# Constant products put between the tensor engine's waits at the head of a two-block transformer kernel

## What is computed

```python
c_act = jax.nn.silu(c)
for l in range(DEPTH):
    mod = (c_act @ ada_w[l] + ada_b[l])[:, None, :]
    sh1, sc1, gt1, sh2, sc2, gt2 = jnp.split(mod, 6, axis=-1)
    h = rms_norm(x, norm_mix[l]) * (1.0 + sc1) + sh1
    x = x + gt1 * hybrid_mixer(h, w_in[l], ...)      # begins with proj = h @ w_in
    ...
```

## Time and profile before

| | |
|---|---|
| Median of three runs | 3062.19 us (3061.9 to 3067.84) |
| The profiled execution: its own time | 3064.68 us |
| Its span, first to last instruction | 3062.9 us |
| PE busy | 2978.7 us, 97% of the span |
| DVE busy | 2351.1 us, 77% |
| Mean granted clock of TensorE | 0.988 of full |

### The profile page before, as it was taken

How to read it: one execution, slowest core, us unless ns; L and a number is a source line. 1 busy time by engine, 2 the same in 40 slices (tenths; PEclk the granted TensorE clock), 3 DMA queues, 4 the chain that set the end, 5 groups by cost and what they waited for, 6 DMA issues and landing times.

```text
span 3062.9 us, 49634 instructions
## 1 busy us (share of the span) xinstructions
PE 2978.7 (97%) x20726; PEld 2665.8 (87%) x20726; DVE 2351.1 (77%) x2670; ACT 1637.7 (53%) x1613; POOL 74.3 (2%) x83
## 2 busy tenths in 40 slices
PE   7999999999999999999999999999989999998999
PEld 7998999999888788788887888899979988986898
DVE  7978698848675888989888888689687646658576
ACT  3445443445553777777777777643334424435543
POOL 0002000000010000000000000000000000100000
PEclk8999999999999999999999999999999999999999
DMA  8650487735303799999999999845325553541353
GB/s 357 255 192 11 176 316 304 264 121 188 142 16 124 280 362 369 362 368 368 364 368 358 371 365 371 305 153 185 130 94 196 181 177 139 205 165 42 129 187 123
DMA packets 130027, 703.09 MB, mean 230 GB/s; under 512 B 11184, under 2 KB 15552, under 8 KB 74048
## 3 DMA queue, kind: packets, MB, share of 16 engines
q1 hardware_dynamic: 118816, 650.30, 58.0%
q0 software_dynamic: 6880, 48.24, 3.9%
q10 hardware_dynamic: 4160, 2.12, 0.3%
HBM read 698.50 MB, written 1.07 MB: 228 GB/s over the span
## 4 chain that ended last, share of the span: by engine, by line
PE 89%; DVE 6%; ACT 2%; DMA 1%; issue 1%; SPq 0%; ACTq 0%; DVEq 0%
PE banks L532 20%; PE banks L533 20%; PE banks L534 20%; PE banks L542 7%; PE banks L543 4%; PE banks L475 3%; DMA ring<-in_wall 1%; DVE big L1446 1%; DVE ring_low L1446 1%; PE banks L643 1%; PE banks L485 1%; PE banks L891 1%; DVE tail L1446 1%; ACT parts L2562 1%; PE banks L555 1%
## 5 line engine op out<-in xcount | busy, mean ns | idle before, releaser
L1446 DVE TENSOR_TENSOR ring_low<-ring,parts 128x2048 fp32r<-128x2048 f32 x589 | 1341.5, 2287 | 281.4 <-ACT parts L2562 252.1
L532 PE MATMUL banks<-parts 128*128 128x256 f32 (+1 forms) x3360 | 1063.1, 316 | 4.2 <-ACT big L2733 2.2
L2562 ACT ACTIVATE parts<-ring 128x2048 fp32r<-128x2048 f32 x253 | 484.7, 1916 | 731.7 <-PE banks L534 495.4
L2668 ACT ACTIVATE parts<-ring 128x2048 fp32r<-128x2048 f32 x336 | 644.7, 1919 | 215.3 <-DMA ring<-in_wall 210.2
L534 PE MATMUL banks<-parts,ring_low 128*128 128x256 f32 x2464 | 694.1, 282 | 0.0
L532 PEld LDWEIGHTS banks<-parts 128*128 128x128 f32 x3360 | 634.7, 189 | 44.7 <-issue 3.3
L533 PE MATMUL banks<-tail_parts,parts 128*128 128x256 f32 x2032 | 573.3, 282 | 0.0
L534 PEld LDWEIGHTS banks<-parts,ring_low 128*128 128x128 f32 x2464 | 465.9, 189 | 0.0
L533 PEld LDWEIGHTS banks<-tail_parts,parts 128*128 128x128 f32 x2032 | 383.2, 189 | 1.9 <-issue 1.9
L542 PE MATMUL banks<-tail_parts,parts 128*128 128x512 f32 x1008 | 354.9, 394 | 1.6 <-DVE big L1496 1.1
L534 PE MATMUL banks<-parts,tail_parts 128*128 128x512 f32 x896 | 352.6, 394 | 0.0
(11 more groups left out here) (478 smaller groups left out, 3771.6 us busy)
## 6 DMA issues: line engine op xcount, KB each, us to landing
ring<-in_wall SPq DMA_DIRECT2D x616, 1024.0 KB, 6.5
big<-in_wall POOLq DMA_DIRECT2D x40, 1024.0 KB, 5.5
big<-in_w_k POOLq DMA_DIRECT2D x1, 2048.0 KB, 8.3
big<-in_w_v POOLq DMA_DIRECT2D x1, 2048.0 KB, 14.5
big<-bias_table ACTq DMA_DIRECT2D x2, 1024.0 KB, 7.2
constants<-in_con SPq DMA_DIRECT2D x1, 1249.5 KB, 9.0
x<-in_x SPq DMA_DIRECT2D x1, 1024.0 KB, 6.8
big<-big POOLq DMA_DIRECT2D x16, 64.0 KB, 4.8
```

Of the source, the lines that this page charges most:

```text
L532: pe.matmul(o, high, in_high, start=start, stop=False, **kw)
L1446: return ve.tensor_tensor(out, a, b, op)
L2562: act(parts(w_high(room, n), UNIT), ring[n % RING][:, :], ACT.Copy).then_inc(sem("w_high"), 1)
L2668: act(parts(slot_at(q), UNIT), ring[r][:, :], ACT.Copy).then_inc(sem("x_high"), 1)
```

## The change

`ada()` gets a helper that multiplies `EPS_ONES` by itself into bank 5, which nothing reads there (each product starts its own sum and ends it). 24 such products stand ahead of everything, six ahead of the wait for unit 1, and six ahead of each wait for the units 4, 5, 6 and 7: 54 products, 108 records. Nothing else is changed.

```diff
+            def keep_busy(count):
+
+                for _ in range(count):
+                    pe.matmul(bank[5][:, 0:P], EPS_ONES[:, :], EPS_ONES[:, :], start=True, stop=True)
+
             def ada():
 
+                pe.wait_ge(sem("eps_set"), 1)
+                keep_busy(24)
                 for n in range(FIRST):
+                    if n == 1:
+                        keep_busy(6)
                     if n == 2:
                         norm(0, 7)
+                    if n > 3:
+                        keep_busy(6)
                     pe.wait_ge(sem("weighted"), (n + 1) * KT)
                     for t in range(2):
                         for chain in range(2):
```

## The result

The changed kernel takes 3068.49 us in the median of 20 runs (3063.38 to 3075.48), the kernel before 3063.01 in 20 (3058.5 to 3067.84). The medians differ by 5.5 us; the ratio, estimated from all executions, is 1.0015, with a 95% interval of 1.0009 to 1.0021: 2.8 to 6.4 us slower, and clear of noise. In the experiments further down one execution of the kernel before, of 29, took 10867.86 us at a mean granted clock of 0.509, and no ratio counts it. The profiled execution took 3070.84 us, its span is 3069.0 and its mean granted clock 0.985.

What follows compares the result with a forecast made beforehand. The first slice's head delays the end in full, limited by DVE's weighing and PE's low-clock norm. PE then becomes the limit: +5.0 us, 0.8 of it from the norm, projections 0; 3062.2 + 5.0 = 3067.2, range 3062.8 to 3069.8.

Steps and rivals of the forecast that it cites:

- The opening burst: First 24 products: wait for x, run from 9.0 to 16.8; unit 0 done at 17.7, unit 2 weighed from 17.8.
- Absorbed by the idle time: Ahead of `modulation`: DVE's 3.54 us idle takes nearly all of a 3.4 us delay; `modulation` comes +0.8 us later.
- Units 4 to 7: After the norm: groups at the lower clock make PE the limit; unit 7 done at 45.1 instead of 39.9.
- The first projection: End of the head: 3.24 us of copy and `ring_low`, then start at 50.3 instead of 45.27, +5.0 us.
- The projections' clock: First projections: start at the lower clock again, as before; taken as 0, range 0 to 0.9 us lost.
- The sum: Whole kernel: +5.0 us on the median of 3062.2 gives 3067.2, 0.16% slower; forecast chance 0.66.
- That the clock wouldn't rise between the groups: Units 4 to 7: clock stays low; five groups of 1.72 and three of 2.58 us make 16.3 us.
- The first rival: Units 4 to 7: clock holds at full, DVE stays the limit; +1.5 us, 3063.7; chance 0.18.
- The constants do lift the clock: Opening burst: the rival denied this, burst low throughout to 19.3; +14.6 us, 3076.8; chance 0.06.
- The Trainium skill's rule of idle gaps: Head: if only idle time lowers the clock, full clock to the projections; +0.8, -1.9, 3061.1; rival's chance 0.06.

Runs made afterwards that it cites:

- the early variant: Changed kernel with the opening 24 products moved ahead of PE's wait for x, all groups kept: 3071.45 us, ratio 1.0015 to the kernel before.
- the first experiment: Changed kernel with only the opening 24 products kept, all five groups of six removed: 3067.57 us, ratio 1.0009 to the kernel before.
- the two courses of one program: Unchanged repeats of the early variant, one profiled execution each: a slow one of 3068.42 us and a quick one of 3062.49 us.
- half the length: Changed kernel with three products instead of six ahead of each of units 4 to 7: 3069.99 us, ratio 1.0012 to the kernel before.
- the fourth profile of the early variant: Unchanged repeat of the early variant, one profiled execution: 3062.49 us, first projection at 43.63.
- the held version: Changed kernel, opening 24 ahead of the wait for x, sixteen ahead of unit 1, groups in every later PE pause: 3059.61 us, ratio 0.9985.

## Why the prediction was right

**The opening burst.** Predicted from 9.0, ended at 16.8; it ran from 9.12 to 17.26. Unit 0 done at 17.7: 18.04. Unit 2 weighed from 17.8: 18.15. The premise that the wait for `x` stands ahead of it is shown by the bracket of its row, and by the early variants, where it starts at 1.10.

**Absorbed by the idle time.** DVE's 3.78 us of waiting ahead of unit 2 came out of the 3.54 ahead of `modulation`, of which 0.84 is left. `modulation` at 24.6 predicted, 24.89 measured, +1.1 for +0.8. The working had both the burst and the six products ahead of unit 1 in that term without parting them, and the expectation for the first experiment gave the whole to the burst. Most of it belongs to the six: they take 1.42 us ahead of the norm (17.90 to 19.32). Without them, by an estimate from the changed kernel's rows, DVE would be the limit, with unit 3 weighed at about 24.0 and `modulation` right behind, +0.2.

**Units 4 to 7.** The group ended at 29.7 where I had chosen 28.8 between 28.5 and 30.5; the clock fell within it, so the level of this one term was between the ends as priced. The rest of the chain was 16.3 us in the working and is 16.0 (29.7 to 45.70); a group and a unit together took 4.27 us (31.05 to 35.32) for 4.3. Unit 7 was predicted at 45.1 and is done at 45.70, and DVE waits 4.21 us for it. The experiments with these groups alone, with half of them, and with the two courses of one program carry this step.

**The first projection.** 50.3 predicted, 50.53 measured; +5.3 for +5.0. The 3.24 us behind the 128x16 pair were 3.0, since ACT's part was done early.

**The projections' clock** stayed low for at least 4.8 us (50.5 to 55.3) against 3.9, worth 0.5 of the 0.9 that I had kept for the range.

**The sum.** +5.0 on the median predicted, a ratio worth +4.6 (2.8 to 6.4) measured, and +5.5 between the medians. The landmarks carry the account; that the time follows the head to half a microsecond is partly luck, since "the opening burst alone" and "half the length" came out slower (2.8 and 3.7 us by their ratios) than their heads (-0.8 and +1.9). The remark that less than 0.2% can hardly be told from no change was wrong: with 20 executions of each the interval is 0.06% to either side.

**What was too strong.** That the clock wouldn't rise between the groups. It held for the changed kernel's profiled execution and for four others with groups of six, but the fourth profile of the early variant shows a rise behind the first group, and a third of that variant's executions were of the quick kind. The first rival, to which I gave 0.18, isn't something that a kernel has or hasn't; it is a course that some executions take. For the changed kernel itself no execution of that kind was profiled, and its 20 times show no gap at the low end, so how often it takes it stays open. Three of the 20 (3074.83 to 3075.48) lie 3.4 us above the others, and no profile shows one of these either.

**The rivals.** The constants do lift the clock: 48 records in 8.14 us, where all at the lower level would be 10.3. The Trainium skill's rule of idle gaps ("TensorE: Matmul & The Clock Gate", section "Why this matters for your kernels") doesn't fit the head: PE was without any pause from 27.4 to 49.2 us, and the clock was at 0.50 from 30 to 50 us and mostly already from 28.

## What to carry to other kernels

Filler work waits in its engine's order like any other: look up every wait that stands ahead of it, and price it at the lower clock, because it is met at that clock just where it is thought to be needed. A group that fits into a pause at full and not at half the clock makes the engine that was waited on the one that waits, and PE busy at the lower level, with narrow products in between, may not lift it again. Either it is dense from the first wait to the last, as in the version that won 0.15%, or it is better left out behind the norm. The early burst with sixteen ahead of unit 1 won 3.0 us in the head as well, with a ratio that doesn't yet tell it from no change.

## What the runs showed of the hardware

A busy PE doesn't get the full clock by being busy: with 19.16 of 20 us busy, in groups of 128x128 and in 128x1 and 128x16 products by turns, the granted clock stayed at 0.50, while in the held version, with the same kinds of products by turns and 15 of 15 us busy from 25 to 40 us, it stayed at 1.00, where it had been from the start of the norm. The held version also has more constant products (70 against 30 behind the burst), so the runs don't part how much of this is the denser filling and how much the level that it came from. The same program took one course or the other from one execution to the next, 5.9 us apart. And unchanged code of 3015 to 3024 us varied by 8 us between profiled executions, 7.3 of them in one stretch of 145 to 152 us with the granted clock at 0.96 or 0.92.
